# Two half-width passes for each product of the feature-major stage

## What the kernel computes

```python
h = rms_norm(x, norm1_g) * (1 + scale1) + shift1
z = h @ w_in                                  # 8192 columns
cb, cc, cx, q, k, v, gc, ga = jnp.split(z, idx, axis=-1)
y_conv = (cb * short_conv3(cc * cx, conv_w)) @ w_conv_out
o = diff_attention(rope(rms_norm(q)), rope(rms_norm(k)), v, lam)      # 8 heads
y_attn = rms_norm(o, subln_g) * (1.0 - lam_init) @ w_attn_out
mixed = sigmoid(gc) * y_conv + sigmoid(ga) * y_attn
x = x + gate1 * (mixed @ w_o)
x = x + gate2 * hier_moe(rms_norm(x, norm2_g) * (1 + scale2) + shift2, ...)   # 16 experts, 2 for each token
```

## Time and profile before

| | us |
|---|---|
| median of 3 runs | 1277.82 (1275.99 to 1280.12) |
| span of the profiled execution | 1276.5 |
| PE busy | 1234.5 (97%) |
| PEld busy | 775.1 (61%) |
| DVE busy | 582.5 (46%) |
| POOL busy | 370.3 (29%) |
| ACT busy | 232.8 (18%) |

### The profile page before, as it was taken

The page is one execution under the profiler, slowest core; times in us unless marked ns, Lnnn a source line. Parts: engine busy times, 40 slices in busy tenths (PEclk is TensorE's granted clock), DMA queues, the critical chain, the costliest instruction groups (busy, mean ns, idle before and its releaser), DMA issues.

```text
span 1276.5 us, 12824 instructions
## 1 busy us (share of the span) xinstructions
PE 1234.5 (97%) x4912; PEld 775.1 (61%) x4913; DVE 582.5 (46%) x1097; ACT 232.8 (18%) x482; POOL 370.3 (29%) x313
## 2 busy tenths in 40 slices
PE   4999999999999999999999999999899999999996
PEld 1567677777777777777777777555444444444442
DVE  2553378455766671663343354466422323132223
ACT  3221256123560001001100100112111011010100
POOL 0465500576002342343333330000312313222222
PEclk9899999999999999999999999999999999999998
DMA  9844220012201111111111154412997988888761
GB/s 353 291 175 156 74 75 1 17 66 75 75 1 65 68 67 66 66 66 66 66 66 66 66 214 165 165 66 103 379 422 297 366 319 362 336 336 354 304 238 34
DMA packets 59994, 209.07 MB, mean 164 GB/s; under 512 B 9568, under 2 KB 10144, under 8 KB 53792
## 3 DMA queue, kind: packets, MB, share of 16 engines
q1 hardware_dynamic: 47328, 186.25, 38.1%
q0 software_dynamic: 12288, 21.52, 4.7%
q10 hardware_dynamic: 320, 0.53, 0.1%
HBM read 208.24 MB, written 23.10 MB: 181 GB/s over the span
## 4 chain that ended last, share of the span: by engine, by line
PE 95%; DVE 2%; DMA 1%; ACT 0%; issue 0%; POOL 0%; SPq 0%; POOLq 0%; DVEq 0%
PE psum L1954 33%; PE psum L2111 17%; PE psum L1760 11%; PE psum L2130 9%; PE psum L2018 5%; PE psum L1738 4%; PE psum L1862 3%; PE psum L1680 3%; PE psum L1922 3%; PE psum L1896 1%; PE psum L2091 1%; DMA weight_ring<-in_w_ada 1%; PE psum L1775 1%; PE psum L2118 1%; PE psum L1902 1%; PE psum L2033 1%
## 5 line engine op out<-in xcount | busy, mean ns | idle before, releaser
L1954 PE MATMUL psum<-arena,weight_ring 128*128 128x320 f32 x928 | 256.9, 432 | 0.0
L2111 PE MATMUL psum<-weight_ring,arena 128*128 128x512 f32 x512 | 222.6, 592 | 0.3 <-ACT arena L1017 0.3
L1954 PEld LDWEIGHTS psum<-arena,weight_ring 128*128 128x128 f32 x928 | 175.9, 190 | 72.7
L638 POOL TENSOR_TENSOR weight_ring<-weight_ring 128x512 f32<-128x512 f32 x80 | 106.2, 1328 | 353.0 <-DMA weight_ring<-in_w_in 199.5
L1954 PE MATMUL psum<-x,weight_ring 128*128 128x320 f32 x640 | 179.5, 432 | 0.0
L2111 PEld LDWEIGHTS psum<-weight_ring,arena 128*128 128x128 f32 x512 | 96.1, 190 | 115.3 <-issue 114.7
L1954 PEld LDWEIGHTS psum<-x,weight_ring 128*128 128x128 f32 x640 | 121.1, 190 | 49.6
L2130 PE MATMUL psum<-arena 128*128 128x512 f32 x256 | 112.6, 593 | 0.7 <-ACT arena L1025 0.7
L639 POOL TENSOR_TENSOR weight_ring<-weight_ring 128x512 f32<-128x512 f32 x80 | 109.7, 1372 | 0.0
L1357 DVE TENSOR_TENSOR arena<-psum,arena 128x320 f32<-128x320 f32 x124 | 59.5, 488 | 92.3 <-PE psum L1954 91.8
L1622 DVE SCALAR_TENSOR_TENSOR arena<-psum,ropeC,arena 128x512 f32<-128x512 f32 x16 | 12.0, 751 | 188.5 <-ACT arena L1021 188.5
(11 more groups left out here) (268 smaller groups left out, 1335.3 us busy)
## 6 DMA issues: line engine op xcount, KB each, us to landing
weight_ring<-in_w SPq DMA_DIRECT2D x32, 2048.0 KB, 11.9
weight_ring<-in_w_in SPq DMA_DIRECT2D x16, 2048.0 KB, 8.1
arena<-in_w SPq DMA_DIRECT2D x16, 2048.0 KB, 11.9
arena<-in_w_ada SPq DMA_DIRECT2D x6, 2048.0 KB, 11.8
weight_ring<-in_w_ada SPq DMA_DIRECT2D x8, 1024.0 KB, 14.4
x<-in_x_sample SPq DMA_DIRECT2D x2, 2048.0 KB, 12.4
weight_ring<-in_w_conv_out SPq DMA_DIRECT2D x2, 2048.0 KB, 8.1
weight_ring<-in_w_attn_out SPq DMA_DIRECT2D x2, 2048.0 KB, 8.1
```

The lines of the kernel that those rows point to most:

```text
L638: nc.gpsimd.tensor_tensor(out[:, 0:2], a_[:, 0:2], b_[:, 0:2], op)
L1954: last = mm(product_psum(q, name), w[:, k, :], src[:, k, :], start=(k == 0), stop=(k == 3))
L2111: last = mm(psum[:, 1024 + 512 * j:1536 + 512 * j], xgT[:, t, :], w[:, t, :], start=(t == 0), stop=(t == KT - 1))
```

## The change

The two loops of one product are exchanged for a pair: for each half of the 320 token columns, the four `k` blocks are run over 160 columns. The two halves lie side by side in the same bank. The same 128 x 128 weight block is now given to two matmul calls, four calls apart.

```diff
-                for k in range(4):
-                    last = mm(product_psum(q, name), w[:, k, :], src[:, k, :], start=(k == 0), stop=(k == 3))
+                for half in range(2):
+                    part = slice(HALF // 2 * half, HALF // 2 * (half + 1))
+                    for k in range(4):
+                        last = mm(product_psum(q, name)[:, part], w[:, k, :], src[:, k, part], start=(k == 0), stop=(k == 3))
                 last.then_inc(s_fp, 1)
```

## The result

The changed kernel takes 1283.62 us (median of 7 runs, 1281.48 to 1285.22), the kernel before 1278.05 us (7 runs). The ratio is 1.0037, with a 95% interval of 1.0025 to 1.0049, so +3.2 to +6.3 us: slower by 0.4%, with an interval that lies above 1. The profiled execution has a span of 1280.2 us, 3.7 us more than that of before, and took 1282.04 us in all, 1.8 us around the span.

A forecast was written before the change was run, and what follows sets the result against it. PE was taken to bound the kernel, through its stream of matmul passes at L1954. 1568 passes at 269.2 ns (422.1 us) become 3136 at 135.8 (426.0 us): +3.9 us, 1281.7 us on the median; range 1279.5 to 1289.

The forecast's parts named there:

- slope: Price of a pass per column on PE: 0.834 ns, two clocks of 2.4 GHz, from 512 to 256 columns.
- seam: Cost of each PE pass whatever its width, 2 to 3 ns; 1568 more of 2.5 ns give +3.9 us.
- The upper bound of 137.7 ns: Pass price at 160 columns, interpolated between measured 128 and 256 columns; 431.8 us for the stage, +9.8 us.
- the floor: Least price of a narrow PE pass, about 112 ns, set by the next pass's weight load and not by columns.
- the hidden load: In the stage of L1954, the next pass's weight load stays behind the 135.8 ns stream, 24 ns above 112.
- The strict overlap rule: Skill's statement that weight loads overlap running matmuls only where the row group differs; every load here would stand bare.
- A: Rival at L1954: each added weight load is bare and costs 0.112 us, +176 us, 1453 us; chance 2%.
- B: Rival in the stage: PE's instructions come too slowly, 86 ns a record, +118 us, 1396 us; chance 5%.
- C: Rival at product starts: first load not fetched ahead, 104 ns for each of 196, 1302 us with seams; chance 7%.
- D: Rival behind the stage: a wait takes up the seams, or they don't double; down to +0, 1277.8 us; chance 6%.
- more than 10 us of cover: In the stage, PE wants a PSUM bank back only six products later, over 10 us after DVE or ACT read.
- a sign that it is wrong: Later stages changing their length, or a pitch off by more than 2 ns, would show the prediction wrong.

The follow-up runs named there:

- the quarters: Against the changed kernel, each product in four passes over 80 columns in place of two over 160; 1554.83 us, ratio 1.2165 to the kernel before.
- the four further splits: Edits of changed kernel: 80-column passes, 1554.83 us; 208 and 112 columns, 1306.16 us; of kernel before: experts' 512-column lines in three, 1282.08 us, or four, 1291.47 us.

## Why the prediction was right

**The bound.** PE has no idle time in the stage in either profile, and the stage's lengthening went into the end whole.

**The terms.** Forecast: 135.8 ns a pass, +3.9 us. Measured: 135.8 ns and +3.92 us. Three widths of the trace before fixed a slope and a seam, and the fourth width fell on them. The upper bound of 137.7 ns, a straight line from 128 to 256 columns, was too careful, because 128 columns lie on the floor, 2.5 ns above the line. Two slips in the working changed nothing: 431.8 us is 9.7 and not 9.8 above 422.1, and the stage before took a record each 132 ns (3227 in 426.8 us) and not 135.

**The floor and the hidden load.** 80 columns cost 111.7 ns, as 20 and 128 did. This is the part of the argument on which the size of the change hung: 160 columns keep 24 ns over the floor. The floor is measured; that the load sets it is the likeliest reading and not shown by itself. The strict overlap rule of the Trainium skill ("TensorE: Matmul & The Clock Gate", section "The mechanism") doesn't hold for these full-height passes, whose loads last 190 ns and which still come each 135.8 ns; a load in the background fits.

**The rivals.** A (bare loads) would have shown 176 us and didn't. B (supply of instructions) fell with the quarters, and the 3136 added instructions show as 12 more packets of instruction fetch, 36 to 48, at no cost. C (lost cover) didn't show with six banks, whose stage has no microsecond beyond its seams; with two, both forms pay its 104 ns alike at the few products that wait. D (a wait behind that takes up the seams) didn't happen: everything behind the stage is as long as its scatter in the kernel before.

**What was wrong and did no harm.** The prediction gave the PSUM banks more than 10 us of cover, from the totals of what DVE and ACT wait; a total says nothing of the one late read, and the least cover was 1.8 us. It also named a change in the length of the later stages as a sign that it is wrong. They did change, by 2.3 us, but the kernel before changes by 2.5 us against itself, so the sign could not tell. The cover still held, and the mechanism stands; on the banks that was luck.

**The size in the medians.** The medians say +5.6 and +4.5 us, the profiles' stage +3.9. The intervals, 1.0025 to 1.0049 and 1.0020 to 1.0045, hold 1.0031. What the medians have beyond 3.9 us is not shown to be of the change; start and router wander by 2 to 3 us from one execution to the next. The forecast of 1281.7 us also stood on a median of 1277.82, which over more runs is 1278.05. The 1.3 us that I put between span and median compared a median with the span of another execution; the profiled one of after has 1.8 us around its span, and so have the later ones of before. It entered the comparison alone and not the sum.

## What to carry to other kernels

Read the pitch, not the duration: with the chain's long pieces (time over count) at three widths, a float32 pass that keeps PE busy was max(columns x 0.833 + 2.5, 111.7) ns here at the full clock, and that priced the four further splits to within 1%. Splitting a stream of matmuls costs its seams only, as long as each part by itself is above about 131 columns ((111.7 - 2.5) / 0.833; an estimate, as no run lies between 128 and 160). Below that each pass costs the floor, whatever its neighbours are. To see an effect of 0.3%, compare the stage between two fixed instructions of the profile, which repeated within 0.01 us, and not the medians, which have an interval of 3 us. To know the cover of a buffer, look for its latest reader, not for the total of the reader's waits.

## What the runs showed beyond that

The stretch of the router is the kernel's source of scatter: 106.2 to 110.0 us over all ten profiles. In each of them the granted clock is down there for 3.4 to 10.2 us in all, in different places; the three longest stretches, 109.8 to 110.0 us, are those in which it stays down for 10.2 us behind the wait of L2044. What sets the place stays open. In the windows of both feature-major stages, where PE is never idle, the clock is 1.00.
